# Merge of the attention groups in an encoder layer: coefficient rows repeated by DMA instead of by a selector matrix

## The reference

```python
for g, (w, dil) in enumerate(ATTN_PATTERNS):            # 3 groups of 4 heads, 64 channels a head
    o, l = dilated_window_attention(q[:, :, hs], k[:, :, hs], v[:, :, hs], w, dil)
    outs.append(o)                                      # (B, S, 4, 64)
    lses.append(l)                                      # (B, S, 4), log of the softmax sums
alpha = jax.nn.softmax(jnp.stack(lses, axis=0), axis=0) # one coefficient per group, token and head
merged = jnp.sum(alpha[..., None] * outs, axis=0).reshape(B, S, ATTN_OUT_WIDTH)
...
x = x + (g_a * a + g_b * (merged @ w_up_attn)) @ w_out  # a: the pooling mixer's branch
```

## Time and profile before

| what | value |
|---|---|
| median of 3 executions | 2494.0 us (2493.11 to 2495.1) |
| the profiled execution, its own time | 2492.61 us |
| its span, first to last instruction | 2490.8 us |
| PE busy | 2475.9 us (99%) |
| DVE, ACT, POOL busy | 1281.0, 1028.2, 1685.6 us (51%, 41%, 68%) |
| granted TensorE clock, mean | 0.999 |
| mean DMA rate | 144 GB/s |

### The profile page before, as it was taken

One profiled execution on the slowest core, in us unless ns is written; L12 is line 12 of the kernel. 1 busy time (PEld: TensorE's weight loads), 2 busy tenths in 40 slices (PEclk: granted clock), 3 DMA queues, 4 the chain that ended last, 5 costly groups with the idle time before them and its releaser, 6 DMA issues. The chain is left out here.

```text
span 2490.8 us, 33219 instructions
## 1 busy us (share of the span) xinstructions
PE 2475.9 (99%) x12044; PEld 2039.5 (82%) x12044; DVE 1281.0 (51%) x1739; ACT 1028.2 (41%) x1984; POOL 1685.6 (68%) x1247
## 2 busy tenths in 40 slices
PE   9999999999999999999999999999999999999998
PEld 8878778888888888888888888788888888888887
DVE  7874455645322222388957745466462222224768
ACT  6224553445323323346552255434453323333445
POOL 6665457445888888756787754573468888886543
PEclk9999999999999999999999999999999999999999
DMA  7444565552233333474363345556523333335544
GB/s 255 126 142 148 166 179 167 196 209 93 81 117 100 102 106 109 153 246 143 108 193 106 117 150 164 170 167 210 194 77 106 102 102 102 115 98 181 179 130 141
DMA packets 330272, 357.95 MB, mean 144 GB/s; under 512 B 39168, under 2 KB 234368, under 8 KB 328576
## 3 DMA queue, kind: packets, MB, share of 16 engines
q1 hardware_dynamic: 328528, 352.58, 45.0%
q10 hardware_dynamic: 1584, 3.26, 0.4%
HBM read 254.39 MB, written 101.38 MB: 143 GB/s over the span
## 5 line engine op out<-in xcount | busy, mean ns | idle before, releaser
L1340 PE MATMUL ps<-S,t_hi 128*128 128x512 f32 (+1 forms) x2268 | 890.0, 392 | 1.8 <-DVE v L2567 1.4
L1342 PE MATMUL ps<-S,t_lo 128*128 128x512 f32 (+1 forms) x2268 | 879.7, 388 | 0.0
L1341 PE MATMUL ps<-S,t_hi 128*128 128x512 f32 (+1 forms) x2268 | 879.0, 388 | 0.0
L1340 PEld LDWEIGHTS ps<-S,t_hi 128*128 128x128 f32 x2268 | 425.8, 188 | 93.3 <-issue 6.5
L1342 PEld LDWEIGHTS ps<-S,t_lo 128*128 128x128 f32 x2268 | 425.8, 188 | 87.6
L1341 PEld LDWEIGHTS ps<-S,t_hi 128*128 128x128 f32 x2268 | 426.1, 188 | 85.0 <-issue 1.0
L1095 POOL TENSOR_TENSOR t_lo<-wraw,t_hi 128x512 fp32r<-128x512 f32 x170 | 227.4, 1338 | 189.9 <-ACT t_hi L1896 187.4
L1095 POOL TENSOR_TENSOR t_lo<-wraw_ff,t_hi 128x512 fp32r<-128x512 f32 x225 | 289.1, 1286 | 78.6 <-ACT t_hi L1896 69.4
L1095 POOL TENSOR_TENSOR t_lo<-R,t_hi 128x512 fp32r<-128x512 f32 x154 | 217.9, 1419 | 177.4 <-ACT t_hi L1896 177.4
L1896 ACT CAST t_hi<-wraw_ff 128x512 fp32r<-128x512 f32 x225 | 139.9, 623 | 364.4 <-PE ps L1342 363.2
L1340 PE MATMUL ps<-t_hi,d_hi 128*128 128x512 f32 x616 | 240.5, 390 | 0.0
(11 more groups left out here) (230 smaller groups left out, 3994.8 us busy)
## 6 DMA issues: line engine op xcount, KB each, us to landing
d_raw<-d_rows SPq DMA_DIRECT2D x154, 256.0 KB, 2.8
d_rows<-act_f SPq DMA_DIRECT2D x110, 256.0 KB, 2.2
wraw_ff<-w_ffn_up SPq DMA_DIRECT2D x44, 512.0 KB, 4.7
R<-w_ffn_down SPq DMA_DIRECT2D x88, 256.0 KB, 3.2
sp_rows<-gst SPq DMA_DIRECT2D x80, 256.0 KB, 2.3
wraw_ff<-w_ffn_gate SPq DMA_DIRECT2D x40, 512.0 KB, 5.0
wraw<-w_in SPq DMA_DIRECT2D x38, 512.0 KB, 6.1
wo_raw<-w_out SPq DMA_DIRECT2D x36, 512.0 KB, 3.9
```

Of the source, the lines that this page charges most:

```text
L1340: nc.tensor.matmul(o_ps, w[0], r[0], start=begins, stop=False, skip_group_check=True)
L1341: nc.tensor.matmul(o_ps, w[0], r[1], start=False, stop=False, skip_group_check=True)
L1342: return nc.tensor.matmul(o_ps, w[1], r[0], start=False, stop=ends, skip_group_check=True)
```

## The change

The coefficients are not rounded and split, but transposed in float32 (12 columns instead of 24). ACT evicts them to 12 partitions of `coefT` without waiting for a clearing. SP stores these 12 rows of 4 KB to DRAM (`store_coefficients`, into `d_rows`, which is otherwise unused at that time) and loads them back with each row repeated over 64 partitions: two DMAs of 256 KB fill one tile `spread_coef[g]` (128 x 1024) for a group, for all tokens and one q. There are three such tiles, filled for q = 0 at once, and refilled for q = 1 as soon as the multiplies of q = 0 have read them. `merge_step` multiplies by the SBUF tile instead of by a PSUM bank. The 12 products per sequence, `sel`, the split and the clearing are gone. The four loads of `wu_raw` now wait for `ct_read` = 12 instead of `ct_full` = 12, since the tiles share memory with `wu_raw`.

```diff
+            def coef_rows():
+                return d_rows[0, 0, 0:24].rearrange("(r h) c -> r (h c)", h=2)
+
+            def store_coefficients(s):
+
+                sp.wait_ge(cT_ready, due("cT_ready", s, 1))
+                sp.dma_start(coef_rows(), coefT[0:12, :]).then_inc(coef_stored, 16)
+
+            def load_coefficients(s, q, g):
+
+                sp.wait_ge(coef_stored, due("coef_stored", s, 1))
+                if q:
+                    sp.wait_ge(ct_read, due("ct_read", s, GROUPS + g + 1))
+                for e in range(2):
+                    sp.dma_start(spread_coef[g][HEAD * e:HEAD * e + HEAD, :], coef_rows()[4 * g + 2 * q + e].partition_broadcast(HEAD)
+                                 ).then_inc(spread_in[g], 16)
...
+                    if m == SPREAD0 - 1:
+                        store_coefficients(s)
+                        for g in range(GROUPS):
+                            load_coefficients(s, 0, g)
+                    if m == SPREAD0 + 2:
+                        load_coefficients(s, 1, 0)
                     if m == SPREAD0 + 3:
+                        for g in range(1, GROUPS):
+                            load_coefficients(s, 1, g)
                         sp.wait_ge(mix_stored, due("mix_stored", s, 8))
                         load_mixed(s, range(3), 1)
                     if m == SPREAD0 + 6:
-                        sp.wait_ge(ct_full, due("ct_full", s, 12))
+                        sp.wait_ge(ct_read, due("ct_read", s, 12))
                         load_up(s, 0)
                         load_up(s, 1)
...
-                if m == SPREAD0 + 1:
-                    clear_coefficients(s)
...
-                        if 0 <= m - SPREAD0 < len(MERGE) // 2:
-                            spread_coefficients(s, 2 * (m - SPREAD0))
-                            spread_coefficients(s, 2 * (m - SPREAD0) + 1)
...
             def evict_coefficients(s):
 
                 act.wait_ge(cT_full, due("cT_full", s, 1))
-                for r in range(2):
-                    act.wait_ge(o_stored[r], due(f"o_stored{r}", s, 6))
-                act.wait_ge(cT_zero, due("cT_zero", s, 1))
-                nc.scalar.copy(coefT[0:24, :], ps[0:24, 4:6, :].rearrange("r b c -> r (b c)")).then_inc(cT_ready, 1)
+                nc.scalar.copy(coefT[0:12, :], ps[0:12, 4:6, :].rearrange("r b c -> r (b c)")).then_inc(cT_ready, 1)
...
                 q, h, g = MERGE[f]
-                spread, o = ps[:, 4 + (f + 2) % 4, :], by_residue(2 * g + q, h)
+                spread, o = spread_coef[g][:, half(h)], by_residue(2 * g + q, h)
                 if f % 6 == 0:
                     dve.wait_ge(ot_in[q], due(f"ot_in{q}", s, 3))
                 if f == 0:
                     dve.wait_ge(mix_stored, due("mix_stored", s, 8))
-                dve.wait_ge(ct_full, due("ct_full", s, f + 1))
+                dve.wait_ge(spread_in[g], due(f"spread_in{g}", s, 2 * q + 2))
                 V_.tensor_tensor(natural(mT[q][:, half(h)], g) if g == 0 else o, o, natural(spread, g), ALU.mult
                                  ).then_inc(ct_read, 1)
...
                     if m == MERGE0 - 1:
-                        make_selector(s)
                         merge_differences(s)
                     if m == MERGE0:
                         merge_coefficients(s)
-                    if m == MERGE0 + 2:
-                        split_coefficients(s)
```

More of the change, by code:

```diff
@@ L235 @@
     "pooled_ready": 8, "mix_hi_ready": 4,
-    "mixed_ready": 4, "diff_ready": 1, "weight_ready": 1, "coef_ready": 1, "coef_hi": 1, "coef_split": 1, "sel_ready": 1, "cT_zero": 1, "cT_full": 1, "cT_ready": 1,
-    "ct_full": 12, "ct_read": 12, "two_merged": 4, "merged": 2,
+    "mixed_ready": 4, "diff_ready": 1, "weight_ready": 1, "coef_ready": 1, "coef_turned": 1, "cT_full": 1, "cT_ready": 1,
+    "ct_read": 12, "two_merged": 4, "merged": 2,
     "mhi_ready": 2, "mT_ready": 2,
@@ L257 @@
 DMA_SEMS.update({f"ml_in{g}": 1 for g in range(4)})
+DMA_SEMS.update({f"spread_in{g}": 4 for g in range(GROUPS)})
 DMA_SEMS.update({f"r_in{r}": 11 for r in range(4)})
@@ L412, in encoder @@
         st_all, mT = at("st_all", XR + 32000, [TT, 6, 4]), [at(f"mT{q}", WX + 4096 + 4096 * q, [T]) for q in range(2)]
-        coef, coefT = at("coef", WX + 19712, [TT, 24], F32R), at("coefT", XR + 27648, [T], F32R)
-        sel = at("sel", XR + 24576, [6, 2, HEAD], F32R)
+        coef, coefT = at("coef", WX + 19712, [TT, 12]), at("coefT", XR + 24576, [T])
+        spread_coef = [at(f"spread_coef{g}", o, [T]) for g, o in enumerate((XR + 24576, EX, EX + 8192))]
         ml = [at(f"ml{g}", XR + o, [T]) for g, o in enumerate((0, 4096, 8192, 12288))]
@@ L498, in encoder @@
         wo_in = [sems[f"wo_in{r}"] for r in range(3)]
+        spread_in = [sems[f"spread_in{g}"] for g in range(GROUPS)]
         xl_in, xh_in, tiles_stored, ml_in, r_in, d_in = (
@@ L1525, in coefficient_transposes @@
                 ins.then_inc(cT_full, 1)
-            def spread_coefficients(s, f):
-                q, h, g = MERGE[f]
-                b = 4 + (f + 2) % 4
-                if f == 0:
-                    pe.wait_ge(sel_ready, due("sel_ready", s, 1))
-                    pe.wait_ge(cT_ready, due("cT_ready", s, 1))
-                bank_read(b)
-                nc.tensor.matmul(ps[:, b, :], sel[:, 2 * g + q, :, :].rearrange("r h e -> r (h e)"), coefT[:, half(h)],
-                                 start=True, stop=True).then_inc(ct_full, 1)
-                last[b] = ("ct_read", s, f + 1)
             def pair_product(s, m, done=1):
@@ L2003, in merge_weights, with order_coefficients @@
                 nc.scalar.activation(d3[:, :, :], d3[:, :, :], ACT.Exp).then_inc(weight_ready, 1)
[L2005 removed]
+            def order_coefficients(s):
                 act.wait_ge(coef_ready, due("coef_ready", s, 1))
                 nc.scalar.copy(coef[:, :, 0:12].rearrange("p t (g x) -> p t g x", x=4),
[L2009 removed]
+                               d3[:, :, :].rearrange("p g (t x) -> p t g x", x=4)).then_inc(coef_turned, 1)
             def evict_coefficients(s):
                 act.wait_ge(cT_full, due("cT_full", s, 1))
[L2014 to L2017 removed]
+                nc.scalar.copy(coefT[0:12, :], ps[0:12, 4:6, :].rearrange("r b c -> r (b c)")).then_inc(cT_ready, 1)
             def merged_hi(s, q):
@@ L2700, in merge_coefficients @@
                                  ).then_inc(coef_ready, 1)
-            def split_coefficients(s):
-                dve.wait_ge(coef_hi, due("coef_hi", s, 1))
-                group = "p t (g x) -> p t g x"
-                V_.tensor_tensor(coef[:, :, 12:24].rearrange(group, x=4), d3[:, :, :].rearrange("p g (t x) -> p t g x", x=4),
-                                 coef[:, :, 0:12].rearrange(group, x=4).bitcast(F32), ALU.subtract).then_inc(coef_split, 1)
-            def make_selector(s):
-                dve.wait_ge(o_full, due("o_full", s, N_QUADS))
-                high, low = (ident_sb[:, c:c + 12].unsqueeze(2).broadcast_to([P, 12, HEAD]) for c in (0, 12))
-                V_.tensor_tensor(sel[:, :, :, :].rearrange("r x h e -> r (x h) e"), high, low, ALU.add
-                                 ).then_inc(sel_ready, 1)
             def merge_step(s, f):
                 q, h, g = MERGE[f]
-                spread, o = ps[:, 4 + (f + 2) % 4, :], by_residue(2 * g + q, h)
+                spread, o = spread_coef[g][:, half(h)], by_residue(2 * g + q, h)
                 if f % 6 == 0:
```

21 lines of the change are left out of this document (7 added, 14 removed).

## The result

| | before | changed kernel |
|---|---|---|
| median | 2494.01 us (2493.11 to 2495.1, 6 executions) | 2513.45 us (2512.73 to 2517.1, 6 executions) |
| the profiled execution, its own time and span | 2492.61, 2490.8 us | 2515.0, 2512.7 us |
| granted TensorE clock, mean | 0.999 | 0.996 |

The ratio is 1.0082 (95% interval 1.0071 to 1.0093). The change costs 19.4 us. The profiled execution of the changed kernel lies 1.5 us above its median, so its rows account for somewhat more than that.

The account below looks back on a forecast made before the run. PE was taken as the bound, busy 2475.9 of 2490.8 us. The second stall, 10.1 us per sequence, absorbed the first and PE's gain: 2 x 10.1 = 20 us on 2492.6, plus 1.4 to the median: 2514 us, range 2502 to 2524.

Parts of the forecast that it names:

- Lock and stride: Merge multiplies: DVE with two SBUF inputs and POOL never run together; 0.59 us unstrided, 0.99 strided; chance as forecast 0.55.
- packed row: Merge: DVE's 13.3 us and POOL's instructions pass one at a time, 25.3 to 26.8 us, twelfth multiply ending about 454.7.
- First stall: Before product 131: PE waits about 9.7 us for v, queued behind the multiplies; product 131 is 7.0 us later.
- Second stall: First up product: wu_raw loads wait for the twelfth multiply; fourth tile at 466.0, 10.1 us later, absorbing the first stall.
- Clock: After PE's wait: rival that PE falls to 1.2 GHz, adding 2.2 to 4.3 us per sequence, 2518 to 2523; chance 0.18.
- Arrival: Coefficient loads before the merge: groups at 428.0, 429.4, 430.8, delay caught up; slow-loads rival 2520 to 2524, chance 0.12.
- PE's gain: PE's stream: twelve selector products leave, 2.72 us per sequence, 5.4 in all.
- the rivals' paragraph: Its faster rival: multiplies run ahead, wu_raw loads go earlier, at best 1.9 of 2.72 us per sequence; chance 0.03.
- PE's narrow margin: First up product before the change: PE only just not held by the wu_raw chain, waiting 0.8 us in two weight loads.

Follow-up runs that it names:

- rows loaded without a store, through PSUM, early weights: Changed kernel with ACT copying coefficients to PSUM for the multiply and early wu_raw loads, but no store, loads reading rows of a weight: 2496.18 us.
- PE kept busy: Changed kernel with early wu_raw loads and 32 matmuls, whose result nobody reads, in front of product 131: 2510.53 us, ratio 1.0065.
- the arrival and the copies alone: Changed kernel, but ACT copies each half of a landed coefficient tile into PSUM and the multiply reads it there: 2500.88 us, ratio 1.0026.

## Why the prediction was right

The forecast was 2514 us, measured were 2513.45. The mechanism was right; that the number came out within 1 us is luck in part, as the terms below show. The runs, in order, give the loss as a ladder of differences to the kernel before:

| kernel | to before | step |
|---|---|---|
| no products, coefficients for nothing | -1.8 us | -1.8 |
| rows loaded without a store, through PSUM, early weights | +1.9 | +3.7: the loads and ACT's copies |
| with the store | +5.3 | +3.4: the hop to DRAM |
| multiply reads SBUF | +18.1 | +12.8: lock and stride |
| weights behind the twelfth multiply | +19.4 | +1.3: late weights |

- **Lock and stride**: the main term, right in kind and size. Its packed row of 25.3 to 26.8 us took 25.8 with the second SBUF input alone, and 25.3 in the changed kernel (429.81 to 455.10), waits for landings included; the twelfth multiply ended at 455.1 for a forecast 454.7. Two errors cancel in that: the row started at 429.8 instead of 428.6, and took 25.3 instead of the 26.1 that the forecast used. It was not packed from its start either: POOL had no work for 4.39 us in front of its first sum. By the rule of the Trainium skill ("SBUF — State Buffer", Who interferes with whom), an exclusive lock, the trace agrees: 2.14 for a `t_lo` of 1.28. No run takes POOL's work away, so that the two take turns is read from where their instructions end; that the second SBUF input makes the loss is shown by experiment, once by adding it (+14.6) and once by taking it away (-13.0; -12.8 between the two kernels with early weights).
- **First stall**: forecast 9.7 us, measured 8.1; product 131 at 455.84 is 7.5 later than before, for a forecast 7.0. The other 1.6 us are there as well: PE waited 1.53 us for the `t_lo` of product 130 just before. "POOL's operands for PE are ready ahead of time" was wrong (2.8 us in all for the three such waits), and it did no harm, since PE would have waited for `v` instead.
- **Second stall**: the moment was right (466.31 for a forecast 466.0), the way there was not. It was to be reached by a wait of 2 to 5 us; the wait was 0.71. From product 131 to the fourth tile PE took 10.5 us, where before it took 7.6: 1.7 of the difference is the slow clock and 1.1 the waits for the third and fourth tile. In the second sequence the clock took 2.8 and left a wait of 0.3 (1713.53). That the stall absorbs the other one, and PE's 2.72, was right. The forecast reached the fourth tile by the loads of `wu_raw`, 11.2 us behind the twelfth multiply, and 11.2 were measured. What it did not see is a second way that is nearly as long, DVE's own stream. In every trace but that of the single large load the fourth tile starts 0.05 to 0.13 us behind DVE's last remainder. This one ends 11.2 to 11.4 us behind the twelfth multiply where the loads wait for it, and still 9.9 to 10.2 in the kernel before, with the second SBUF input alone, and in the changed kernel with early weights, be it alone, with PE kept busy or through PSUM (10.4 to 11.6 in the other three traces). So moving the loads could not have undone the second stall: 1.1 of its 10.4 us are theirs.
- **Clock**: the condition of this rival came true (0.50 behind the wait), its price did not: the clock was back at 1.00 before the fourth tile in both sequences, and what it cost lay in front of the late tile, in the second sequence by a margin of only 0.3 us.
- **Arrival**, a mis-sized term: "some 0.35 each" for an issue was 0.6, "I take 2.8" for the landing was 4.5, and the second and third group came some 2 us apart instead of 1.4. "This delay alone would be caught up" failed: with the lock gone it costs 7 us for both sequences, ACT's copies included. It is not hidden beside the lock either. From the start of the sum before the first multiply to the end of the twelfth it takes 19.0 us before, 21.6 with the arrival and the copies alone, 26.4 with the second SBUF input alone, and 28.7 and 27.8 in the two sequences of the changed kernel. In the sum it did no harm only because the row behind it came out short, as said above.
- **PE's gain**: "5.4 in all: all that this change can give" is 1.8 at best, as the rivals' paragraph half saw (1.9 of 2.72 per sequence). This did not enter the forecast, whose path ran through DVE.
- **The moved wait** alone measured 1.3 us, which fits the rows on PE's narrow margin and isn't clear of noise; in its traces the last remainder ends 11.3 us behind the twelfth multiply instead of 10.1.

## What to carry to other kernels

Before moving an operand from PSUM to SBUF, look at what the other input is and what POOL does beside it: a DVE instruction with two SBUF inputs next to a POOL that is busy for 80% can take about both lengths (0.69 us became up to 1.8 here), and a stride on that input comes on top. An engine that is busy for 100% need not be the bound of a stretch when its neighbours are packed too: take the work out without a substitute first, and see whether the time moves. When two stalls end at nearly the same moment, price them together: taking away the later one alone gave 1.2 us here. And before a stall is put down to loads, look at what stands in the stream of the engine that makes the operand.

## What the runs showed of the hardware that was not expected

- A load that repeats one DRAM row of 4 KB over 64 partitions (256 KB) lands after 4.5 us (median of 24), against 2.9 for the most frequent load of that size in the same kernel (`d_raw`), and takes 0.6 us of SP's queue. Six are issued in a row, and `wu_raw`, of the same size and without repetition, takes 5.4, so that the repetition is the cause is not shown.
- With the same data as one transfer with an outermost dimension of 2, the queue moved 42 GB/s instead of 197 (with two stores in it), and the kernel took 4.2% longer than the one before.
- The multiply with its second input in SBUF takes 0.67 to 0.69 us in order and 1.01 to 1.09 with a stride of 4 or 16 elements, where POOL doesn't work beside it; from PSUM both take 0.66 to 0.70, with POOL or without.
